# Expert outputs scattered by GpSimd, expert 0's weights loaded ahead of routing

## The reference, cut to what matters

```
group_probs = softmax(xf @ w_group + b_group);  p_group, g_idx = top_k(group_probs, 1)
e_logits = (xf @ w_expert + b_expert)[group g_idx];  p_exp, e_local = top_k(softmax(e_logits), 2)
xs = xf[tok]                                   # 2048 rows, sorted by expert, 32 experts
hid = silu(xs @ w1[e]) * (xs @ w3[e])          # 1024 -> 512
ys = (hid @ w2[e]) * gate                      # 512 -> 1024
ffn = segment_sum(ys, tok)                     # two rows of ys for each token
```

## Time and profile before

| | |
|---|---|
| median of 3 runs | 3090.46 us (3088.27 to 3090.53) |
| the profiled execution's own time | 3095.24 us |
| its span | 3093.4 us |
| mean granted TensorE clock | 0.974 |
| TensorE busy | 2912.9 us, 94% |
| VectorE, ScalarE, GpSimd busy | 1174.8, 629.5, 685.1 us |
| DMA, mean over the span | 134 GB/s |

### The profile page before, as it was taken

One profiled execution on the slowest core, in us unless ns is written; L12 is line 12 of the kernel. 1 busy time (PEld: TensorE's weight loads), 2 busy tenths in 40 slices (PEclk: granted clock), 3 DMA queues, 4 the chain that ended last, 5 costly groups with the idle time before them and its releaser, 6 DMA issues.

```text
span 3093.4 us, 30760 instructions
## 1 busy us (share of the span) xinstructions
PE 2912.9 (94%) x12050; PEld 1727.9 (56%) x12050; DVE 1174.8 (38%) x1974; ACT 629.5 (20%) x1351; POOL 685.1 (22%) x528
## 2 busy tenths in 40 slices
PE   7899999789897999999969999999999999999998
PEld 5786544788544666666624455557544444444443
DVE  6714545566213111111134134569734314133142
ACT  4011322322121221211222121147331000000001
POOL 3213342544121000000021000137611122211220
PEclk9999999899998999999989999999999999999999
DMA  8634397000216999999661100030211111111101
GB/s 264 221 51 52 63 217 173 1 28 22 90 77 267 401 427 424 426 427 406 266 246 66 61 1 14 14 106 1 75 41 55 41 41 41 41 55 41 41 27 55
DMA packets 179929, 415.14 MB, mean 134 GB/s; under 512 B 30452, under 2 KB 103604, under 8 KB 170680
## 3 DMA queue, kind: packets, MB, share of 16 engines
q1 hardware_dynamic: 163353, 370.52, 33.9%
q10 hardware_dynamic: 10512, 25.69, 2.6%
q0 software_dynamic: 5904, 16.78, 1.5%
HBM read 366.04 MB, written 59.88 MB: 138 GB/s over the span
## 4 chain that ended last, share of the span: by engine, by line
PE 85%; DVE 6%; DMA 3%; issue 2%; ACT 1%; POOL 1%; SPq 1%; ACTq 0%; POOLq 0%; DVEq 0%
PE bank L3578 27%; PE bank L2345 9%; PE bank L2348 8%; PE bank L1090 5%; PE bank L2775 5%; PE bank L748 4%; PE bank L1757 4%; PE bank L2945 3%; PE bank L232 3%; PE bank L2943 2%; PE bank L883 2%; PE bank L3277 2%; PE bank L3287 2%; PE bank L1660 1%; DMA wa_rest<-in_w_ada 1%
## 5 line engine op out<-in xcount | busy, mean ns | idle before, releaser
L3578 PE MATMUL bank<-w_ff,uT 128*128 128x512 f32 x640 | 276.0, 592 | 0.0
L3578 PE MATMUL bank<-hT,w_ff 128*128 128x512 f32 x512 | 224.3, 596 | 4.3 <-DVE hT L3381 4.3
L3578 PEld LDWEIGHTS bank<-w_ff,uT 128*128 128x128 f32 x640 | 121.6, 190 | 153.1 <-issue 153.1
L3701 DVE TENSOR_TENSOR x_out<-x_out,bank 128x512 f32<-128x512 f32 x140 | 94.5, 686 | 291.7 <-PE bank L3578 291.5
L2345 PE MATMUL bank<-e_w,e_xsT 128*128 128x256 f32 x832 | 184.5, 383 | 1.6 <-DVE e_xsT L2431 1.6
L2348 PE MATMUL bank<-e_w,e_xsT 128*64 128x256 f32 x1408 | 161.0, 389 | 17.8 <-issue 17.8
L2345 PEld LDWEIGHTS bank<-e_w,e_xsT 128*128 128x128 f32 x832 | 158.3, 191 | 32.6 <-issue 11.3
L2775 PE MATMUL bank<-w_gla,nT 128*128 128x512 f32 x384 | 170.5, 604 | 6.0 <-DMA w_gla<-in_w_in 4.7
L1090 PE MATMUL bank<-hT,w_qkv 128*128 128x512 f32 x384 | 169.0, 598 | 3.1 <-DMA w_qkv<-in_w_in 2.4
L3578 PEld LDWEIGHTS bank<-hT,w_ff 128*128 128x128 f32 x512 | 97.5, 191 | 126.3 <-issue 126.1
L3578 PE MATMUL bank<-h_sum,w_ff 128*128 128x512 f32 x384 | 166.1, 592 | 0.0
(11 more groups left out here) (521 smaller groups left out, 4844.0 us busy)
## 6 DMA issues: line engine op xcount, KB each, us to landing
e_w<-in_w SPq DMA_DIRECT2D x105, 2048.0 KB, 29.3
w_ff<-in_w_ff SPq DMA_DIRECT2D x32, 1024.0 KB, 5.2
y_rows<-zero SPq DMA_DIRECT2D x8, 3008.0 KB, 16.2
wa_rest<-in_w_ada SPq DMA_DIRECT2D x32, 512.0 KB, 5.7
y_rows<-e_y ACTq DMA_DIRECT2D x24, 512.0 KB, 9.9
wa<-in_w_ada SPq DMA_DIRECT2D x16, 512.0 KB, 10.7
w_qkv<-in_w_in SPq DMA_DIRECT2D x12, 512.0 KB, 8.0
w_gla<-in_w_in SPq DMA_DIRECT2D x3, 2048.0 KB, 12.9
```

The costliest lines, as they stand in the source:

```text
L3578: t = pe.matmul(bank[:, :], still, moving, start=step in (0, 1, 3) and f == 0, stop=f == 3, skip_group_check=True)
L3701: v.tensor_tensor(dst, dst, k.bank[4 * ((ph + step) % 2) + g][:, :], ALU.add).then_inc(*s.added.up().inc)
```

## The change

GpSimd's indirect DMA now writes the experts' rows, one unit after another, behind the gather that it was to issue then; padding rows have an index out of bounds and are left out. The last unit's rows are written after everything else, from a list copied into a fixed column. ScalarE issues no store any more. The index table `e_idx` is written by VectorE directly, with a second column for the scatter. The first set of weight buffers is now the region from 96 KB to 144 KB; expert 0's w1 is loaded into it at the start of `residual`, its w3 and w2 when the last tile's sum has been made, ahead of the last two stores. The first unit's own load is passed by if its expert is 0. `decay_prefetch` but for its memset is moved behind `mix`.

```diff
 def residual_sync(k, s, b, x_out, xn_out, route_s, route_w, sets):
     ...
     route_load(k, route_s, route_w)
+    experts_first_load(k, s, sets, 0)
     for m in range(NT):
         sy.wait_ge(*s.x_added(2 * (m + 1)))
+        if m == NT - 1:
+            for j in (1, 2):
+                experts_first_load(k, s, sets, j)
         sy.dma_start(x_out[m * P:(m + 1) * P, :], b.x[m][:, :]).then_inc(*s.x_stored.up().inc)
         ...
@@ route_vector
+    v.tensor_scalar(b.rows[:, :], k.c("row")[:, 0:BLOCKS], float(P), k.c("token")[:, 0:1], ALU.mult, ALU.add).then_inc(*V.up().inc)
     ...
     v.wait_ge(*s.places_read(1))
-    v.tensor_scalar(tokens[:, 0:BLOCKS], k.bank[3][:, 0:BLOCKS], float(NO_TOKEN), None, ALU.add).then_inc(*V.up().inc)
-    v.memset(tokens[:, BLOCKS:], 0).then_inc(*V.up().inc)
+    v.tensor_scalar(tokens[:, 0:BLOCKS, 0:1].squeeze(2), k.bank[3][:, 0:BLOCKS], float(NO_TOKEN), None, ALU.add).then_inc(*V.up().inc)
+    v.memset(tokens[:, BLOCKS:, 0:1], 0).then_inc(*V.up().inc)
+    v.memset(tokens[:, BLOCKS:, 1:2], NO_ROW).then_inc(*V.up().inc)
+    v.tensor_scalar(b.free[:, :], k.bank[3][:, 0:BLOCKS], 0.0, float(NO_ROW), ALU.is_ge, ALU.mult).then_inc(*V.up().inc)
+    v.wait_ge(*V.now())
+    v.tensor_tensor(tokens[:, 0:BLOCKS, 1:2].squeeze(2), b.free[:, :], b.rows[:, :], ALU.add).then_inc(*V.up().inc)
@@ experts_sets, experts_first_load
+    return [[... w1, w3, w2 at n_at(48 * n) ...] for n in (2, 0, 1)]
+    k.nc.sync.dma_start(sets[0][j][:, :, :], experts_source(k.io, j, slice(0, 1))).then_inc(*s.first_set_got.up().inc)
@@ experts_sync
     sy.wait_ge(*known)
+    sy.wait_ge(*first_got)
@@ experts_load
+    if u == 0:
+        there = which[0] > 0
@@ experts_gpsimd
-    g.tensor_copy(b.idx[:, :, 0:1].squeeze(2), tokens[:, :]).then_inc(*s.idx_ready.up().inc)
-    g.wait_ge(*s.idx_ready(1))
     ...
+    experts_scatter_last(k, s, b, ys)
+SCATTER_BEHIND = ROWS_AHEAD + 2
+def experts_scatter_last(k, s, b, ys):
+    g.wait_ge(*s.y_out_a(BLOCKS))
+    g.wait_ge(*s.y_out_v(BLOCKS))
+    g.wait_ge(*s.last_listed(1))
+    g.indirect_dma_start(out=ys[:, :], out_offset=bass.IndirectOffsetOnAxis(ap=b.idx[:, 0, 2:3], axis=0), in_=b.y[1][:, :],
+                         in_offset=None, bounds_check=BLOCKS * P - 1, oob_is_err=False).then_inc(*s.y_stored_last.up().inc)
+    g.wait_ge(*s.y_stored_last(1))
+def experts_scatter(k, s, b, ys, at):
+    g, n = k.nc.gpsimd, at % 2
+    g.wait_ge(*s.y_out_a(at + 1))
+    g.wait_ge(*s.y_out_v(at + 1))
+    g.indirect_dma_start(out=ys[:, :], out_offset=bass.IndirectOffsetOnAxis(ap=b.idx[:, UNITS[at][0], 1:2], axis=0), in_=b.y[n][:, :], ...)
@@ experts_gather_group
+    if at >= SCATTER_BEHIND:
+        experts_scatter(k, s, b, ys, at - SCATTER_BEHIND)
     experts_gather(k, s, b, xn, at)
     ...
     with g.Else():
+        for u in range(max(at - SCATTER_BEHIND + 1, 0), at - 1):
+            experts_scatter(k, s, b, ys, u)
+        experts_last_rows(k, s, b, at - 1)
         experts_gathers_done(k, s, at + 1)
+        experts_scatters_done(k, s, at - 1)
@@ experts_scalar
-        a.wait_ge(*s.y_out_a(at + 1))
-        a.wait_ge(*s.y_out_v(at + 1))
-        a.dma_start(ys[UNITS[at][0] * P:(UNITS[at][0] + 1) * P, :], b.y[n][:, :]).then_inc(*stored[n].up().inc)
     ...
-    for n in range(2):
-        a.wait_ge(*stored[n].now())
@@ build
     mix_begin(k, mix_s, mix_b, x_rows[0], y_rows)
-    decay_prefetch(k, decay_s, decay_b)
+    decay_clear(k, decay_s, decay_b)
     near = near_areas(k)
     mix(k, mix_s, mix_b, x_rows[0], x_rows[1], y_rows)
+    decay_prefetch(k, decay_s, decay_b)
```

More of the change, by code:

```diff
@@ L1833, in residual_scalar @@
                 a.activation(hT[:, f, (m - 1) * P:m * P], src, ACT.Identity, scale=affine[:, 2, f:f + 1], bias=affine[:, 3, f:f + 1]).then_inc(*s.half_0_out.up().inc)
-Route = namedtuple("Route", "wr br lg eq gp top ix ixf sel hot both a1 a2 a3 earlier cnt low left upto0 upto1 first lines whole blk ef place w2 row_of blk_of parts hp hb pos lT fresh below")
+Route = namedtuple("Route", "wr br lg eq gp top ix ixf sel hot both a1 a2 a3 earlier cnt low left upto0 upto1 first lines whole blk ef place w2 row_of blk_of parts hp hb pos lT fresh below free rows")
 NL = GROUPS + NE
 NO_TOKEN = 4 * T
+NO_ROW = 1 << 16
 RouteWeights = namedtuple("RouteWeights", "w b")
@@ L1870, in route @@
               late("w2", NT, NE), late("row_of", NT, 2), late("blk_of", NT, 2), late("parts", 2, NT, 2, dt=U32), wait("hp", NT, 2, P), wait("hb", NT, 2, BLOCKS),
-              late("pos", NT, 2), early("lT", BANK), early("fresh", SAME - 1), late("below", NT))
+              late("pos", NT, 2), early("lT", BANK), early("fresh", SAME - 1), late("below", NT), late("free", BLOCKS), late("rows", BLOCKS))
     s = k.on("columns_made columns_out logits_made group_shifted group_exp ratio_ready ratio_exp chosen_ready ranks_made counts_ready counts_laid places_ready places_read")
@@ L2149, with experts_sets @@
 UNIT_OF_LOAD = [u for u, (_, loads, _) in enumerate(UNITS) for _ in loads]
-def experts_pass(k, scale, shift, tokens, experts, known, xn, ys, indices, begin_next):
+def experts_sets(k):
     n_at = lambda kb: N_AT + kb * KB
-    sets = [[k.at(f"e_w{j}_{n}", n_at(48 * n + 16 * j), P, NK, DE) for j in range(2)] + [k.at(f"e_w2_{n}", n_at(48 * n + 32), P, DE // P, D)] for n in range(SETS)]
+    return [[k.at(f"e_w{j}_{n}", n_at(48 * n + 16 * j), P, NK, DE) for j in range(2)] + [k.at(f"e_w2_{n}", n_at(48 * n + 32), P, DE // P, D)] for n in (2, 0, 1)]
@@ L2163, in experts_pass @@
[L2163 to L2164 removed]
+    s = k.on("last_listed up_made half_0_turned hid_turned half_1_turned down_made silu_ready hidT_out half_0_out y_out_a hid_ready half_1_out y_out_v",
+             "up_loaded_0 up_loaded_1 up_loaded_2 gate_loaded_0 gate_loaded_1 gate_loaded_2 down_loaded_0 down_loaded_1 down_loaded_2",
+             "rows_got_0 rows_got_1 rows_got_2 rows_got_3 rows_got_4 rows_got_5 y_stored_0 y_stored_1 y_stored_last")
@@ L2165, in experts_pass @@
+    experts_sync(k, s, b, experts, known, first_got)
+    experts_gpsimd(k, s, b, experts, xn, ys, indices)
     experts_tensor(k, s, b, experts)
-    experts_scalar(k, s, b, experts, scale, shift, ys)
+    experts_scalar(k, s, b, experts, scale, shift)
     experts_vector(k, s, b, experts, scale, shift)
@@ L2172, in experts_pass @@
     k.meet(sync=False, behind=True)
+    for n, signal in enumerate(experts_stored(s)):
+        signal.made = signal.base + len(range(n, BLOCKS, 2))
+    s.last_listed.made = s.last_listed.base + 1
     for signal, step in ((s.half_0_turned, 1), (s.half_1_turned, 1), (s.half_0_out, 4), (s.half_1_out, 4)):
@@ L2198, in experts_loaded, with experts_sync @@
     return (s.up_loaded_0, s.up_loaded_1, s.up_loaded_2), (s.gate_loaded_0, s.gate_loaded_1, s.gate_loaded_2), (s.down_loaded_0, s.down_loaded_1, s.down_loaded_2)
-def experts_sync(k, s, b, experts, known):
+def experts_sync(k, s, b, experts, known, first_got):
     sy = k.nc.sync
     sy.wait_ge(*known)
+    sy.wait_ge(*first_got)
     used = used_blocks(sy, experts)
@@ L2470, in skip @@
         a.sem_inc(s.y_out_a.sem, 1)
-        a.sem_inc(stored[at % 2].sem, 16)
     def rest(at, blocks):
@@ L2478, in rest @@
         a.sem_inc(s.y_out_a.sem, blocks)
-        for n in range(min(blocks, 2)):
-            a.sem_inc(stored[(at + n) % 2].sem, 16 * ((blocks + 1 - n) // 2))
     experts_blocks(a, used, work, skip, rest)
-    for n in range(2):
-        a.wait_ge(*stored[n].now())
 def experts_vector(k, s, b, experts, scale, shift):
```

55 lines of the change are left out of this document (38 added, 17 removed).

## The result

The changed kernel takes 3095.77 us (median; 3089.85 to 3103.29), the kernel before, run beside it, 3091.49. The ratio is 1.0014, with a 95% interval of 1.0007 to 1.0020: slower by 4.3 us, where 3086.5, 4.0 less, was predicted. The time lies within the predicted range, the direction is wrong; both the 4.0 forecast and the 4.3 measured lie under the 6.2 us by which the prediction itself had told a change from none.

The account below looks back on a forecast made before the run. It took the experts to begin bound by TensorE and turn bound by DMA bytes; 0 + 9.4 + 1.8 - 0.5 - 8.7 + 3.2 - 9.2 = -4.0 from the 3090.5 median gave 3086.5 us, range 3077 to 3097.

Parts of the forecast that it names:

- stores held behind the loads: End of residual: last stores land behind w3 and w2 on SyncE's queue, everything later by 9.4 us; bounds 0 and 12.
- route: cold matmul, less copy: Route: projection at the lower clock after idleness, +1.8 us; GpSimd's copy and its first gather's wait gone, -0.5.
- first gather and first blocks: Start of experts: loading expert 0 early saves 0, as TensorE's first unit waits for the gather; bounds -4.3 and 0.
- experts behind the first pair: Experts: the scatter leaves out padding, 4.19 MB less to store, -8.7 us; bounds -10 and 0.
- seam to mix: Experts to mix: mix's first gather waits for the last scatter's landing, the meet and next issue, +3.2 us; bounds +1 and +6.
- mix up to project (1): Mix: with `decay_prefetch` behind it, no wait for `w_gla` and tile 2 of x earlier, -9.2 us; bounds -11 and -4.7.
- The factor 21/24: Experts: share of the scatter's 9.9 us that counts, being stored until the last load is issued; gives 8.7 us.
- The slip past 44.67 us a round: Experts: TensorE's loss against its own pace of 44.67 us per pair and full block, forecast down from 24.8 to about 16.
- SyncE now stands behind a full queue: Rival at mix: third chunk and x tile 2 land as late, saving only -4.7 for -9.2, 3091 us; chance 0.16.
- fewer DMAs compete: Argument for the rival that the preload pays at the first gather, -4.3 us, 3082; chance 0.15.
- the reading by which the stores might have landed early: Rival at residual's end: stores not held by the loads, so 9.4 + 1.8 fall away, 3075 us; chance 0.10.
- the slower rival: Experts: scatter landing passes 22 us, ScalarE waits for `e_y`, the 8.7 are lost and 5 more, 3100 us; chance 0.12.

Follow-up runs that it names:

- e5: Changed kernel with the last unit's scatter issued by GpSimd behind the meet that ends the experts, not ahead of it; 3089.94 us, 0.9999.
- e9: Changed kernel without the early load, load 1's w2 issued first, the last unit's rows stored by ScalarE with a plain DMA; 3078.36 us, 0.9962.
- e11: Changed kernel without the early load and with `decay_prefetch` back ahead of mix, so only the scatter is left; 3095.81 us, 1.0016.
- e12: Changed kernel, expert 0's w3 and w2 behind residual's last two stores, load 2's w2 first, last rows stored by ScalarE with plain DMA; 3072.25 us, 0.9947.
- e8: Changed kernel with in-bounds indices for padding rows too, so the scatter writes all 128 rows of a block; one run, 3097.12 us.
- e4: Kernel before with `decay_prefetch` moved behind the mix loads and nothing else; 3083.95 us, 0.9978.
- e2: Changed kernel with expert 0's w3 and w2 issued behind the last two stores of residual; 3089.24 us, 0.9998.
- e6: Kernel before with unit 1's w2 issued ahead of its w1 and w3, nothing else; 3086.69 us, 0.9987.
- e3: Changed kernel with GpSimd's wait for the last scatter moved from ahead of the meet to behind it; 3092.88 us, 1.0008.
- e10: Kernel before with two edits, `decay_prefetch` behind the mix loads and unit 1's w2 ahead of its w1 and w3; 3080.45 us, 0.9967.
- e1: Changed kernel run again with nothing changed; 3094.49 us, 1.0015.
- e7: Changed kernel without the early load, so unit 0 loads its own weights; 3089.92 us, 0.9995.

## Why the prediction was wrong, step by step

The terms beside what the stages show (us; after less before):

```
                                 predicted   measured
stores held behind the loads       +9.4       +10.0
route: cold matmul, less copy      +1.3        -0.1
first gather and first blocks       0          -5.7
experts behind the first pair      -8.7        -4.7
seam to mix                        +3.2        +8.2
mix up to project (1)              -9.2        -6.0
all behind it                       0          +3.0
sum                                -4.0        +4.7
```

**The seam is the step that failed.** The scatter was issued 4.2 us after the last product (predicted 4.8) and was on the chain for 6.21 us (predicted 4.5 to 5.5; SyncE had issued 1 MB for mix just ahead of it). Then I had written "the meet and the next issue take 0.8", and they took 5.0, of which 4.07 are GpSimd's drain. I had put that drain at nothing, since in before it stands on no chain: GpSimd came to the meet long ahead of the others, and its 2.19 us were hidden. With the wait for the last scatter GpSimd comes last, and all engines wait for its drain. e5 and e9 take the 4.07 off the chain by two different edits, in both of which the drain is as long but early, and e11 shows it in a kernel that holds nothing but the scatter. My upper bound of +6 was too low: I bounded only the landing. Why the drain takes 4.07 us and not 2.19 stays open. Since the meet before, GpSimd had issued 25 indirect DMAs in before and 48 or 49 in after, e5, e9 and e12; nothing was tried that would tell this from another cause.

The seam is 5.0 of the 8.7 us by which the sum is off, and with it as forecast the change would have been worth -0.3 us, nearly nothing (e5, without the drain on the chain, measures 0.9999). Experts, mix and what lies behind mix fall short by 4.0, 3.2 and 3.0 more. The gain at the first gather, 5.7 us that no term had, made up for part of this. Without it the time would be near 3101.5, outside the range, so that it lies inside is luck.

**Experts, -4.7 for -8.7.** The mechanism is right (e8). The factor 21/24 was not: a byte saved is worth its time only while the DMA engines set the pace. Where the stage begins, the share is 0.93 of full in after; where it ends, it is 0.85 and then 0.43 in these windows of after, while the same windows of before, where the stage ends 8.7 us later, have 0.89 and 0.66:

```profile
1445.00:1491.80 46.80, 45.16 (x267) 30.81 (x268) 5.80 (x14) 9.63 (x20) 1.95 (x2) 1.00 0.85 347
1491.80:1536.50 44.70, 44.67 (x265) 28.95 (x264) 5.79 (x14) 9.64 (x20) 2.16 (x3) 1.00 0.43 178
```

So of 9.9 us of bytes 4.7 were worth something, 0.47 where I took 0.87. How the rest divides over those stretches was not tried. The slip past 44.67 us a round went from 24.8 to 511.5 - 491.4 = 20.1; "about 16" was forecast.

**Mix, -6.0 for -9.2.** `w_gla` is no longer waited for to speak of, but the rival "SyncE now stands behind a full queue" is half true. These rows answer to the earlier trace rows:

```profile
1560.47 7.03 SPq L2647 DMA_DIRECT2D w_gla<-in_w_in  x2
...
1567.56 11.45 SPq L2640 DMA_DIRECT2D x_tile<-x_rows  x2
```

SyncE still stands for 6.58 us at the third chunk, and tile 2 of x, issued at 1567.56, lands at 1588.9: 37.0 us after mix's first gather, where I had 34.6 (1587 against 1552.37) and before has 43.6. In e4 SyncE stands there for 4.34 us, and the stage gives 8.5 of the 9.2. Over the eleven profiles with this edit it gives 6.0 to 8.5 us; what sets it within that span was not tried.

**The gather, -5.7 for 0.** The gain lay just beyond my lower bound of -4.3, since the first blocks gave 1.6 more (44.2 for 45.8): behind the shorter wait they ran at a granted clock of 1.00, where before stood at 0.89 (the windows above). The rival that named it ("fewer DMAs compete") had the right sign for a wrong reason: with equally few the gather took 11.94 (e2), and with all of them 7.73 (e6). In the changed kernel the gain is luck, not a merit of the edit.

**What held.** The stores: 13.07 us to the landing, +10.0, and e2 gives it back. The Trainium skill (DMA: Bandwidth & Descriptors, section Queues, rings and completion order) has each queue's descriptors consumed in ring order, and so it was here; the reading by which the stores might have landed early is not borne out by this trace. The cold matmul: 3.63 us for 1.94; but the placement products of the routing (L1937) ran warmer than before, two groups of 16 in 1.98 and 3.61 us where before has 32 in 7.06, so route as a whole lost nothing. The scatters in the loop: issued in 977 to 1017 ns with VectorE at work, landing in at most 11.7 us, so that the slower rival (a landing over 22 us) was refuted by 10 us, and neither did GpSimd's issues stretch. But VectorE's instructions from 1000 to 1500 us all read a `bank`, so the copy within SBUF by which the prediction weighed this did not arise. The early load by itself: nothing.

**Behind mix**, +3.0 us came that no term held, 0.9 up to the gate and 2.1 behind it. No code differs there. Its rows, after first, show the granted clock: in the first 20 us of the decay stage it is 0.74 in after and 0.83 in before, and the gate's 16 matmuls take 8.48 us (L2912) for 6.02 (L2834).

```profile
1761.10:1781.10 20.00, 19.98 (x38) 8.50 (x39) 7.64 (x9) 14.66 (x10) 0.00 (x0) 0.74 0.30 107
```
```profile
1766.70:1786.70 20.00, 19.98 (x42) 8.60 (x43) 7.45 (x9) 15.84 (x11) 0.00 (x0) 0.83 0.30 106
```

The last stage is 1328.2 to 1328.8 us in nine of the profiles and 1326.7 to 1327.0 in the others, which include e2, e3 and e10 with `decay_prefetch` moved as in after. In all nine the granted clock of the first 20 us from the gate on is 0.74, in all five it is 0.83. So the 2.1 us go with that clock; what decides it stays open, and it is not that edit alone.

## What to carry to other kernels

Price a new DMA at a seam by all that stands between its landing and the next issue, the drain of the engine that waits for it above all. A drain that stands on no chain in the trace at hand has a length all the same, and shows it once that engine comes last. So let GpSimd come to a meeting early, and send a stage's last store from an engine whose drain is short. An early load pays only if the queue it goes through has no store behind it that someone waits for, and here it showed a gain only where something else had made the start earlier. Where small transfers of one queue must pass a bulk load of another, order the bulk so that its small packets are in flight then.

## What the runs showed of the hardware

- GpSimd's drain at the end of the experts takes 4.07 us behind the landing of its own last scatter (the same in after, e1, e2, e7, e8 and e11). It takes 4.06 to 4.08 us as well when it begins some 3 us after the last landing and stands on no chain (e5, e9, e12), and 2.19 us in before, behind gathers alone. With the scatter still in flight it ends 2.0 us behind the landing (e3).
- The same gather of 4 KB rows lands in 10.97 to 11.94 us mostly beside 16 KB packets of another queue and in 7.64 to 8.19 us mostly beside 4 KB packets, with the DMA engines full in both (429 GB/s in before, 409 in e6).
- A store of 0.5 MB issued behind two loads of 2.1 MB on one queue took 13.07 us to land, against 2.6.
